# A mixture-of-experts kernel on one Trainium2 core: the gathers of the third and fourth pass moved ahead of the 16 list stores in GpSimd's order

## The chip, the core and the metric

The kernel runs on one core of one Trainium2 chip. The core has TensorE (matrix products, PE in the profile), VectorE (DVE), ScalarE (ACT), GpSimd (POOL) and SyncE (SP), and 16 DMA engines that carry the transfers that SyncE, ScalarE and GpSimd issue. The metric is the device time of one execution in microseconds (us); lower is better. One execution under the hardware profiler gives the trace that is read here.

## What is computed

Two transformer-like blocks on 512 tokens of 1024 features. The part that matters here is the mixture of experts that ends the first block: each token goes to 4 of 32 experts, an expert is a product with a 1024 x 2048 matrix, a clipped gated activation and a product with a 1024 x 1024 matrix, and the results come back weighted by the router's gates.

```
logits = xf @ w_router + b_router
top_val, top_idx = lax.top_k(logits, 4)
gates = softmax(top_val)
...
hu = xb @ w_up[e] + b_up[e]
x_glu = minimum(hu[:, :D_FF], 7.0); x_lin = clip(hu[:, D_FF:], -7.0, 7.0)
act = x_glu * sigmoid(1.702 * x_glu) * (x_lin + 1.0)
y = act @ w_down[e] + b_down[e]
...
x = x + gate2 * sum over a token's 4 experts of gate * y
```

Ahead of it stand an adaptive norm, a gated delta rule, a sliding-window attention and their output product; behind it a second block of attention, two feed-forward nets of 4096 features and a recurrent net. All weights and activations are float32.

## The kernel before

The program is written engine by engine: each engine has its own list of instructions and runs it in order; semaphores tie them together. The weights of the experts (12 MB each, some 400 MB in all) stream from HBM through six slots of 2 MB in `slots`. SyncE issues the loads (`load`, L165): each waits until TensorE has freed the slot it goes to.

**Routing.** `route_dve` (L1294 to L1434) ranks the experts by their number of tokens and works out, on VectorE, four tables: `xsl` (which row of `h2_dram` each place of an expert takes, ready with the semaphore `places` at L1380), `ysl` (where its result goes), `sloti` (for each of the 16 token-and-choice columns its place in a list by expert, L1413, ready with `route_step` 6) and `tab` (the experts of the left-over blocks and where their list starts, L1433, ready with `blocks_listed`). The last needs a short product on TensorE, `route_blocks_pe`, which runs behind the first pass.

**Passes.** The experts by rank are worked through in 31 passes in the fixed order `RANKS = (14, 15, 0, 27, 28, 16, 1, ...)`. A rank has a fixed capacity in units of 32 tokens: passes 0 and 1 (ranks 14, 15) have 2 units, pass 2 (rank 0) has 6, passes 3 and 4 (ranks 27, 28) have 1, pass 5 has 2, pass 6 (rank 1) has 5. Two units make one quad, and each quad is one gather of 64 rows of 4 KB. Tokens that don't fit an expert's capacity go to left-over blocks behind the passes; these read their tokens and their result's places from `list_dram`.

**TensorE.** `moe_pe` does `turn_x(0)`, and then for each pass i: `up(i)` (L1645, L1647), `turn_x(i + 1)` (L1621: it waits for the gather of pass i + 1 and transposes its rows), `down(i - 1)` (L1681 to L1693), `turn_act(i)` (L1659). VectorE and ScalarE carry the activation, and VectorE copies each quad's result out of PSUM (`y_out`, L1816 to L1820). So pass 2 is gathered for `turn_x(2)`, which stands between `up(1)` and `down(0)`.

**GpSimd.** `moe_pool` issues every gather (`moe_gather`, L1545), every scatter of results (L1585) and the list (L1573): 16 indirect stores of 128 rows of 12 bytes each into `list_dram`. Buffer i % 4 of `xg` takes the rows of pass i, so the gathers of passes 0 to 3 need no buffer to be freed; the gather of pass i + 4 stands at the head of step i of the loop that follows and waits for `xg_free`. `settle` (L1533 to L1536) is a one-element addition and a drain: the next instruction of GpSimd starts when the engine has nothing under way. It stands at the head of each `moe_gather`. The list is needed late: L1588 waits for it four passes from the end.

The buffer of pass 2 is `work[:, 7168:8192]`, whose first half is also `ohs`, read last by VectorE at L1411, ahead of `route_step` 6. The buffer of pass 3 is `work[:, 0:1024]`, which holds routing tables until `blocks_listed`.

Of the kernel before, what the change touches and what calls it, by code (L numbers as in the profile page):

```python
# [107 lines left out]
def build(nc, A, out, dbg=None):  # L108
# [3 lines left out]
    def S(name):  # L112
        if name not in sems:
            sems[name] = ctx.enter_context(nc.semaphore(name))
        return sems[name]

    with ctx:
# [1343 lines left out]
        def quads(i):  # L1461

            return [(q, min(UNITS[RANKS[i]] - 2 * q, 2), QBASE[RANKS[i]] + q) for q in range(QUADS[RANKS[i]])]
# [69 lines left out]
        def settle(g):  # L1533

            g.tensor_tensor(tick[:, 1:2], tick[:, 0:1], tick[:, 0:1], ALU.add)
            g.drain()  # L1536

        def moe_gather(g, i):
            if i >= 4:
                g.wait_ge(S("xg_free"), i - 3)  # L1540
            settle(g)
            for q, units, at in quads(i):
                n = units * UNIT
                to = xg[i % 4][q * 64:q * 64 + n] if q < 2 else xg_rest[0:n]
                g.indirect_dma_start(to, None, h2_dram, bass.IndirectOffsetOnAxis(ap=xsl[0:n, at:at + 1], axis=0),  # L1545
                                     bounds_check=T - 1, oob_is_err=False).then_inc(S(f"xg_in{i % 4}"), 16)

        def block_list(g, b, n):

            row = g.value_load(tab[0:1, bass.ds(b + (E + MAXO), 1)] if n is None else tab[0:1, E + MAXO + b:E + MAXO + b + 1], min_val=0, max_val=LROWS - BLK)  # L1550
            g.dma_start(idxA[:], list_dram[bass.ds(row, BLK), :]).then_inc(S("block_list"), 16)
            rows = list_dram[bass.ds(row, BLK), :].rearrange("(u r) c -> u r c", u=2)
            for u in range(2):
                for h in range(2):
                    g.dma_start(idxB[64 * u + 32 * h:64 * u + 32 * h + 32], rows[u, :, 1 + h:2 + h]).then_inc(S("block_list"), 16)

        def block_gather(g):
            settle(g)
            g.indirect_dma_start(xg[3][0:BLK], None, h2_dram, bass.IndirectOffsetOnAxis(ap=idxA[:, 0:1], axis=0)).then_inc(S("block_x"), 16)

        def moe_pool(g):
            g.memset(tick[:], 0.0)
            g.drain()
            g.wait_ge(S("places"), 1)
            g.wait_ge(S("h2_out"), 16 * TT)
            moe_gather(g, 0)
            g.wait_ge(S("biases"), 1)
            moe_gather(g, 1)
            g.wait_ge(S("list_filled"), 16)
            g.wait_ge(S("route_step"), 6)  # L1570
            settle(g)
            for j in range(TT * TOPK):
                g.indirect_dma_start(list_dram, bass.IndirectOffsetOnAxis(ap=sloti[:, j:j + 1], axis=0),  # L1573
                                     pairs[:, 3 * j:3 * j + 3], None, bounds_check=E * T - 1, oob_is_err=False).then_inc(S("list_out"), 16)
            moe_gather(g, 2)
            g.wait_ge(S("blocks_listed"), 1)
            moe_gather(g, 3)
            for i in range(NPASS):
                if i + 4 < NPASS:
                    moe_gather(g, i + 4)  # L1580
                for q, units, at in quads(i):
                    d, n = up_piece[i] + q, units * 2 * UNIT
                    g.wait_ge(S("y_ready"), d + 1)
                    settle(g)
                    g.indirect_dma_start(y2_dram, bass.IndirectOffsetOnAxis(ap=ysl[0:n, at:at + 1], axis=0), ybuf[0:n, d % 2], None,  # L1585
                                         bounds_check=2 * T * TOPK - 1, oob_is_err=False).then_inc(S(f"y_out{d % 2}"), 16)
                if i == NPASS - 4:
                    g.wait_ge(S("list_out"), 16 * TT * TOPK)  # L1588
                    block_list(g, 0, 0)
                    g.wait_ge(S("xg_free"), NPASS - 3)  # L1590
                    g.wait_ge(S("block_list"), 80)
                    block_gather(g)
            nb = g.value_load(tab[0:1, E + 2 * MAXO:E + 2 * MAXO + 1], min_val=1, max_val=MAXO)
            with g.Fori(0, nb) as b:
                g.wait_ge(S("y_ready"), b + (UPS + 1))
                settle(g)
                g.indirect_dma_start(y2_dram, bass.IndirectOffsetOnAxis(ap=idxB[:], axis=0), ybuf[:, UPS % 2], None,
                                     bounds_check=2 * T * TOPK - 1, oob_is_err=False).then_inc(S("block_y"), 16)
                g.wait_ge(S("block_y"), b * 16 + 16)
                settle(g)  # L1600
                g.drain().then_inc(S("block_done"), 1)
                block_list(g, b + 1, None)
                g.wait_ge(S("block_list"), b * 80 + 160)
                block_gather(g)
                g.wait_ge(S("block_x"), b * 16 + 32)
            for p in range(2):
                g.wait_ge(S(f"y_out{p}"), 16 * ((UPS + 1 - p) // 2))
# [900 lines left out]
        with nc.Block() as block:  # L2508
# [113 lines left out]
            @block.gpsimd  # L2622
            def _(g):
                def end():
                    meet(g, "pool")
                ada_pool(g); end()
                mixer_loads(g); ada_bias_loads(g); end()
                dn_moves(g); end()
                second_mods(g); mod_turned_loads(g)
                g.wait_ge(S("turned_out"), TURNED + PIECE["w"] + TT)  # L2630
                route_fill(g); route_loads(g)
                g.wait_ge(S("w_sum"), TT)
                gate_load(g, 5 * D); end()
                moe_pool(g); end()
                at_loads(g)
                g.wait_ge(S("x_done"), 1)
                gate_load(g, mods(0, 0)[2]); end()
                ln_loads(g, "a", 0, 0)
                g.wait_ge(S("x_done"), 2)
                gate_load(g, mods(0, 1)[2])  # L2640
                ln_loads(g, "b", 0, 1)
                g.wait_ge(S("x_done"), 3)
                gate_load(g, mods(1, 0)[2])
                rnn_small(g); rnn_gate_loads(g, 0); end()
                rnn2_pool(g); end()
                rnn3_loads(g); ln_loads(g, "c", 1, 0)
                g.wait_ge(S("x_done"), 4)
                gate_load(g, mods(1, 1)[2])
                ln_loads(g, "d", 1, 1); end()
# [32 lines left out]
```

## Time and profile before

| | us |
|---|---|
| median of 3 runs | 3620.05 |
| lowest and highest of them | 3616.89, 3629.53 |
| the profiled execution, time | 3626.3 |
| the profiled execution, span from first to last instruction | 3624.6 |
| TensorE busy, by the span | 3104.3 (86%) |
| VectorE, ScalarE, GpSimd busy | 868.8, 507.1, 237.3 |
| expert weights: 192 loads of 2048 KB | about 400 MB of the 646.73 MB moved |

The experts' stage runs from about 632 us (first load of an expert's weights) to about 1757 us of the span. The busy tenths of the page cut the span into 40 slices of 90.6 us. In the timeline each line is a group of instructions of one kind: start, duration, engine, line, operation, tile written and tiles read, count, and in brackets the idle time ahead of it with what ended it ("issue" is time in which the engine waited for nothing that the profile shows). In a table by stretch the columns are the busy time of each engine with its number of instructions, the granted TensorE clock as a share of the full one (1.00 is 2.4 GHz, 0.50 is 1.2 GHz), the mean busy share of the 16 DMA engines (rounding can take it a little over 1), and GB/s.

### The profile page before, as it was taken

The page shows a single profiled execution, that of the slowest core. Times are in us where ns is not written, and L with a number is a line of the kernel's source. Part 1 is how long each engine was busy: PE and PEld are TensorE (multiplying, and loading weights), DVE is VectorE, ACT ScalarE, POOL GpSimd, SP SyncE. Part 2 cuts the span into 40 slices and gives each one's busy share as a digit, 9 for nine tenths or more (in the row PEclk, how much of TensorE's full clock was granted, in tenths as well). Part 3 has the DMA queues.
Part 4 walks back from the last instruction along what each step waited for, and adds up shares of the span by engine and source line. Part 5 has one row for each costly group of instructions (what it writes and reads, how often), then busy time and mean ns, then how long its engine had stood idle before and what let it go on. Part 6 is the DMA issues. An engine that isn't in the chain of part 4 may idle for free.

```text
span 3624.6 us, 36753 instructions
## 1 busy us (share of the span) xinstructions
PE 3104.3 (86%) x15370; PEld 1381.0 (38%) x15370; DVE 868.8 (24%) x1281; ACT 507.1 (14%) x986; POOL 237.3 (7%) x336
## 2 busy tenths in 40 slices
PE   7999978598999989999575889999699625999998
PEld 3465555232333333333244434444233202444443
DVE  2224243311111111111312220002330671200003
ACT  1030131000000000000112210001100850200001
POOL 0000011201110111101000000000100220000000
PEclk8989967799999999999787899999899757999999
DMA  7108931979999999999500211112220021212110
GB/s 255 47 7 335 340 104 41 342 301 404 381 405 403 402 401 406 405 405 388 227 0 0 105 64 69 69 58 70 72 72 29 17 51 48 91 66 93 69 70 23
DMA packets 167094, 646.73 MB, mean 178 GB/s; under 512 B 20091, under 2 KB 29883, under 8 KB 126337
## 3 DMA queue, kind: packets, MB, share of 16 engines
q1 hardware_dynamic: 151138, 605.91, 43.5%
q0 software_dynamic: 13952, 35.48, 3.3%
q10 hardware_dynamic: 1856, 3.21, 0.3%
q8 instruction: 112, 1.84, 0.2%
q14 instruction: 36, 0.29, 0.0%
HBM read 630.69 MB, written 18.38 MB: 179 GB/s over the span
## 4 chain that ended last, share of the span: by engine, by line
PE 49%; issue 31%; DVE 5%; DMA 5%; POOL 3%; PEld 2%; ACT 2%; POOLq 2%; DVEq 1%; PEldq 0%; ACTq 0%; SPq 0%
PE ps L2177 12%; PE ps L2188 12%; PE ps L2305 6%; PE ps L2481 3%; PE ps L1996 2%; DMA stage<-gate_dram 2%; DMA slots<-in_ada_w_dram 2%; PE ps L2127 2%; PE ps L1104 2%; POOLq L1536 2%; PE ps L314 1%; PE ps L2018 1%; POOL work L1545 1%; PEld ps L434 1%; PE ps L2030 1%
## 5 line engine op out<-in xcount | busy, mean ns | idle before, releaser
L1645 PE MATMUL ps<-slots,hT 128*32 128x512 f32 x5120 | 580.3, 598 | 18.3 <-DMA slots<-in_w_up_dram 7.6
L2177 PE MATMUL ps<-hT,slots 128*128 128x512 f32 x1024 | 448.9, 599 | 13.1 <-ACT hT L975 6.6
L2188 PE MATMUL ps<-slots,work 128*128 128x512 f32 x1024 | 441.8, 593 | 12.2 <-DVE work L2225 12.2
L1645 PEld LDWEIGHTS ps<-slots,hT 128*32 128x32 f32 x5120 | 160.6, 110 | 413.3 <-issue 396.6
L2177 PEld LDWEIGHTS ps<-hT,slots 128*128 128x128 f32 x1024 | 195.3, 192 | 265.9 <-issue 265.9
L2188 PEld LDWEIGHTS ps<-slots,work 128*128 128x128 f32 x1024 | 193.7, 190 | 258.8 <-issue 247.5
L1681 PE MATMUL ps<-slots,work 128*32 128x512 f32 x2112 | 254.5, 608 | 26.1 <-DMA slots<-in_w_down_dram 19.2
L2305 PE MATMUL ps<-hT,slots 128*96 128x512 f32 x512 | 223.7, 598 | 26.3 <-DVEq L2311 24.4
L2481 PE MATMUL ps<-slots,work 96*128 96x512 f32 x256 | 112.6, 602 | 107.4 <-DVE work L2468 107.4
L1796 DVE TENSOR_SCALAR stage<-ps 128x512 f32<-128x512 f32 (+1 forms) x47 | 32.2, 686 | 581.5 <-PE ps L1647 581.1
L1681 PEld LDWEIGHTS ps<-slots,work 128*32 128x32 f32 x2112 | 90.4, 112 | 157.9 <-issue 124.6
L2305 PEld LDWEIGHTS ps<-hT,slots 128*96 128x96 f32 x512 | 83.5, 164 | 166.0 <-issue 166.0
L2216 ACT ACTIVATE stage<-ps 128x512 f32<-128x512 f32 x64 | 38.2, 597 | 759.6 <-PE ps L2177 759.6
L2225 DVE TENSOR_TENSOR work<-stage 128x512 f32<-128x512 f32 x64 | 44.3, 693 | 400.1 <-ACT stage L2216 400.1
L1774 ACT ACTIVATE modA<-stage 128x512 f32<-128x512 f32 (+1 forms) x47 | 29.6, 630 | 639.1 <-DVE stage L1796 639.1
L2481 PEld LDWEIGHTS ps<-slots,work 96*128 96x128 f32 x256 | 49.2, 193 | 169.4 <-issue 169.4
L2238 DVE TENSOR_TENSOR work<-work,ps 128x512 f32<-128x512 f32 x48 | 33.0, 688 | 303.3 <-PE ps L2188 303.3
L1996 PE MATMUL ps<-slots,hT 128*128 128x512 f32 x192 | 85.6, 606 | 3.0 <-ACT hT L975 3.0
L434 PE MATMUL ps<-hT,slots 128*128 128x512 f32 x192 | 85.3, 606 | 1.9 <-DVEq L460 1.4
L1816 DVE COPY modB<-ps 128x512 f32<-128x512 f32 x33 | 22.8, 692 | 247.3 <-PE ps L1684 238.6
L314 PE MATMUL ps<-slots,modA 128*32 128x512 f32 x512 | 65.9, 629 | 14.1 <-DMA slots<-in_ada_w_dram 10.0
L2359 PE MATMUL ps<-work 96*96 96x512 f32 x64 | 42.1, 745 | 39.3 <-ACT slots L2381 24.6
(547 smaller groups left out, 2980.2 us busy)
## 6 DMA issues: line engine op xcount, KB each, us to landing
slots<-in_w_up_dram SPq DMA_DIRECT2D x128, 2048.0 KB, 18.6
slots<-in_w_down_dram SPq DMA_DIRECT2D x64, 2048.0 KB, 17.3
slots<-in_mlp_w_dram SPq DMA_DIRECT2D x32, 2048.0 KB, 8.6
slots<-in_ada_w_dram SPq DMA_DIRECT2D x16, 2048.0 KB, 9.5
slots<-in_w_ada_dram SPq DMA_DIRECT2D x12, 2048.0 KB, 8.6
slots<-in_ada_w_dram SPq DMA_DIRECT2D x16, 1024.0 KB, 7.0
slots<-in_rnn_w_in_dram SPq DMA_DIRECT2D x8, 1536.0 KB, 6.9
slots<-in_w_in_dram SPq DMA_DIRECT2D x5, 2048.0 KB, 17.4
```

The lines of the kernel that those rows point to most:

```text
L314: ins = pe.matmul(ps[32 * j:32 * j + 32, 6 + g % 2], ada_c[:, which, 2 * q + kk], ada_slots[:, s, kk, j * CH:(j + 1) * CH], start=q + kk = ...
L434: ins = pe.matmul(ps[:, m], slots[:, s, k, m * P:(m + 1) * P], hT[:, k, :], start=k == 0, stop=k == KT - 1)
L1104: ins = pe.matmul(ps[:, 2 * (t % 2) + h], hT[:, k, t * P:(t + 1) * P], slots[:, 4 + h, k], start=k == 0, stop=k == KT - 1)
L1536: g.drain()
L1645: ins = pe.matmul(to, x[:, k, unit * UNIT:(unit + 1) * UNIT], upw[s][:, k % 2, col:col + CH], start=k == 0, stop=False)
L1681: ins = pe.matmul(to, actT[:, 4 * q + j, 64 * u + 32 * h:64 * u + 32 * h + 32], downw[sl[h]][:, j, half * CH:(half + 1) * CH], start=k == ...
L1996: ins = pe.matmul(ps[:, i % 4], hT[:, k, t * P:(t + 1) * P], slots[:, s, k], start=k == 0, stop=k == KT - 1)
L2127: ins = pe.matmul(ps[:, 2 * (t % 2) + h], hT[:, k, t * P:(t + 1) * P], slots[:, 4 + h, k], start=k == 0, stop=k == KT - 1)
L2177: ins = pe.matmul(ps[:, m], slots[:, s, k, m * P:(m + 1) * P], hT[:, k, :], start=k == 0, stop=k == KT - 1)
L2188: ins = pe.matmul(ps[:, 4 + 2 * (t % 2) + h], h1T[:, k, t * P:(t + 1) * P], slots[:, 2 + h, k], start=k == 0, stop=k == KT - 1)
L2305: ins = pe.matmul(ps[0:RW, m], slots[:, s, k, m * RW:(m + 1) * RW], hT[:, k, :], start=k == 0, stop=k == KT - 1)
L2481: ins = pe.matmul(ps[:, 2 * (t % 2) + h], xr[:, n, t * P:(t + 1) * P], slots[0:RW, s0 + n // 8, n % 8], start=n == 0, stop=n == RB - 1)
```

## The change

In `moe_pool`, GpSimd's order is changed. Behind the gather of pass 1 it waits for `route_step` 6 and gathers pass 2, waits for `blocks_listed` and gathers pass 3; only then it waits for the list's filling and issues the 16 stores. The single `settle` that stood ahead of the stores goes: each `moe_gather` has its own. Nothing else is changed.

```diff
             moe_gather(g, 0)
             g.wait_ge(S("biases"), 1)
             moe_gather(g, 1)
+            g.wait_ge(S("route_step"), 6)
+            moe_gather(g, 2)
+            g.wait_ge(S("blocks_listed"), 1)
+            moe_gather(g, 3)
             g.wait_ge(S("list_filled"), 16)
-            g.wait_ge(S("route_step"), 6)
-            settle(g)
             for j in range(TT * TOPK):
                 g.indirect_dma_start(list_dram, bass.IndirectOffsetOnAxis(ap=sloti[:, j:j + 1], axis=0),
                                      pairs[:, 3 * j:3 * j + 3], None, bounds_check=E * T - 1, oob_is_err=False).then_inc(S("list_out"), 16)
-            moe_gather(g, 2)
-            g.wait_ge(S("blocks_listed"), 1)
-            moe_gather(g, 3)
             for i in range(NPASS):
                 if i + 4 < NPASS:
                     moe_gather(g, i + 4)
```

## Rows read from the trace of the kernel before

**Rows 1.** The page: granted clock and DMA share in 40 slices.
```profile
PEclk8989967799999999999787899999899757999999
DMA  7108931979999999999500211112220021212110
```

**Rows 2.** Waits of TensorE between 690 and 720 us: total, times, longest.
```profile
PE ps L1621 <- DMA work<-h_dram,xsl: 14.7, 1, 14.7
```

**Rows 3.** Timeline of TensorE, 600 to 860 us: start, duration, what.
```profile
681.12 1.12 PE L1659 MATMUL ps<-ident,work 128*128 128x128 f32 x4 [4.44 <-DVE work L1805]
...
699.07 0.61 PE L1647 MATMUL ps<-work 96*32 96x512 bf16 x8
714.42 3.01 PE L1621 MATMUL ps<-ident,work 128*128 128x128 f32 x16 [14.74 <-DMA work<-h_dram,xsl]
717.69 8.60 PE L1681 MATMUL ps<-slots,work 128*32 128x512 f32 x64 [0.26 <-issue]
...
727.79 42.34 PE L1645 MATMUL ps<-slots,hT 128*32 128x512 f32 x384 [0.41 <-DVE modB L1816]
...
771.64 0.71 PE L1621 MATMUL ps<-ident,work 64*128 64x64 f32 x8
772.61 7.38 PE L1681 MATMUL ps<-slots,work 128*32 128x512 f32 x64 [0.26 <-issue]
...
790.86 0.71 PE L1621 MATMUL ps<-ident,work 64*128 64x64 f32 x8
...
826.06 0.61 PE L1688 MATMUL ps<-work 96*32 96x512 bf16 x2 [2.70 <-DMA slots<-in_w_down_dram]
```

**Rows 4.** Timeline of GpSimd, 560 to 1040 us.
```profile
663.46 0.95 POOL L1545 DMA_INDIRECT work<-h_dram,xsl  x1 [0.92 <-issue]
665.34 0.18 POOL L1535 TENSOR_TENSOR tick<-tick 1x1 f32<-1x1 f32 x1 [0.93 <-DVE work L1414]
673.22 1.04 POOL L1573 DMA_INDIRECT list_dram<-pairs,work  x1 [7.70 <-issue]
...
692.92 0.97 POOL L1573 DMA_INDIRECT list_dram<-pairs,work  x1 [0.30 <-issue]
693.92 0.18 POOL L1535 TENSOR_TENSOR tick<-tick 1x1 f32<-1x1 f32 x1
700.45 0.96 POOL L1545 DMA_INDIRECT work<-h_dram,xsl  x1 [6.35 <-issue]
...
715.34 0.94 POOL L1545 DMA_INDIRECT work<-h_dram,xsl  x1 [11.23 <-issue]
...
719.02 0.91 POOL L1545 DMA_INDIRECT work<-h_dram,xsl  x1 [2.54 <-issue]
```

**Rows 5.** Gathers (L1545) issued from 695 to 708 us: durations ns, time to landing.
```profile
L1545 POOL DMA_INDIRECT work<-h_dram,xsl x3: 933/952/958, 700.4 to 703.0; - x3
...
DMA to landing us min/median/max: 8.7/10.0/11.4
```

**Rows 6.** Timeline of VectorE, 655 to 800 us: last routing step.
```profile
677.72 0.40 DVE L1433 TENSOR_SCALAR tab<-work 1x64 int32<-1x64 f32 x1
```

**Rows 7.** Weight load (L165) issued in 697 to 705 us: its start, time to landing.
```profile
L165 SPq DMA_DIRECT2D slots<-in_w_up_dram x1: 372/372/372, 699.2 to 699.2; - x1
...
DMA to landing us min/median/max: 17.0/17.0/17.0
```

**Rows 8.** Table by stretch of the experts' stage.
```profile
671.00:687.00 16.00, 11.37 (x86) 4.11 (x90) 4.40 (x13) 1.69 (x3) 10.73 (x11) 0.79 1.01 393
```

**Rows 9.** The same table, later stretches.
```profile
712.00:725.00 13.00, 10.21 (x72) 4.57 (x76) 0.00 (x0) 1.76 (x3) 2.03 (x3) 0.69 0.30 92
...
735.00:780.00 45.00, 44.22 (x416) 13.59 (x408) 7.74 (x12) 2.37 (x4) 0.97 (x1) 1.00 0.59 217
780.00:822.00 42.00, 40.36 (x364) 12.84 (x364) 4.79 (x7) 3.14 (x6) 5.93 (x9) 1.00 1.02 389
...
980.00:1200.00 220.00, 210.08 (x1906) 66.77 (x1902) 30.46 (x46) 14.52 (x27) 22.51 (x36) 0.99 1.02 404
```

## Prediction

> **What bounds the kernel now.** I read four views, in this order. First the page in 40 slices: the DMA share is 9 tenths from slice 10 on to slice 19 and lower in slices 7 to 9 [rows 1]. In the experts' stage the weights' stream is the limit, save in a stretch at its head. Second, the waits of TensorE at that head: one wait of 14.7 us, by `turn_x(2)` on the gathered rows of pass 2 [rows 2]. Third, the timelines of TensorE and GpSimd there: `up(1)` ends at about 699.7 (its last group starts at 699.07 and takes 0.61), and `turn_x(2)` starts at 714.42 [rows 3]. GpSimd comes to the gather of pass 2 only at 700.45, because it issues the 16 list stores from 673.22 to 693.9, and the `settle` behind them holds it until about 699.7 [rows 4]. Last, the table by stretch: the DMA engines are busy 0.30 of the time from 712 to 725 and 0.59 from 735 to 780, and 1.02 from 780 on [rows 9]. So up to 780 TensorE sets the time, not the stream: the loads wait for slots that TensorE hasn't freed. From 780 on the stream is full, and at 826.06 TensorE waits for a weight for the first time since [rows 3].
>
> The reader is to see one chain: GpSimd's stores, gather 2, `turn_x(2)`, `down(0)`, `up(2)`, the slots that these free, the loads into them, and then the full stream to the stage's end at 1757.
>
> **The change, part by part.**
>
> *Gather 2, moved ahead.* `route_step` 6 is there when GpSimd has issued gather 1: its `settle` starts at 665.34 and lets the next DMA go at 673.22 [rows 4]. That is where the first store stands now; gather 2 takes its place. Its three DMAs start 1.26 us apart, at 673.2, 674.5 and 675.7. The same three landed 8.7 to 11.4 us after their issue [rows 5], when the DMA engines were full too, so the last lands at about 675.7 + 11.4 = 687.1. The DMA share between 671 and 687 is 1.01 [rows 8], so I take that duration and no shorter one. It is needed at 699.7: there are 12 us in hand. As a bound from above: gather 1, of one DMA, held its `settle` until about 672.4, some 9 us from its issue at 663.46 [rows 4]; three times this in a row gives 673.2 + 27 = 700.2, half a microsecond late. So the wait of 14.7 us goes, or all but 0.5 of it.
>
> *What is late next.* Behind `up(1)`, `turn_x(2)` starts at once, as `turn_x(3)` does at 771.64 behind `up(2)` [rows 3]: 714.42 - 699.7 = 14.7 us earlier. ScalarE must finish one sigmoid before it takes out the transposes, so it may lose some tenths; I take 0 to 0.8. `down(0)` needs weights that were issued before 676 and `up(2)` needs four loads of which the last was issued at 699.2 and landed 17.0 us later, at 716.2 [rows 7]. `up(2)` will start near 711.6 and works through four slots in 42.3 us [rows 3], so it comes to the last one some 32 us in, at 743. No weight is late.
>
> *The clock.* TensorE runs `down(0)` in 8.60 us now, with a granted clock of 0.69 on average over 712 to 725, that is partly at the 1.2 GHz level, behind its 14.7 us of idleness; the same 64 products at 772.61 take 7.38 with the clock at 1.00 [rows 3, 9]. Without the pause `down(0)` gains 1.2 us. A pause of 4.44 us at 681 stays as it is [rows 3]. The clock's gain is between 0 (if the transposes' short pauses bring it down anyway) and 1.5; I take 1.2.
>
> *The sum at `up(2)`.* 14.7 + 1.2 + 0.3 for the transposes' own speed = 16.2 us earlier: 727.8 becomes 711.6. Bounds: 13.9 (0.8 lost on ScalarE, nothing from the clock) and 16.8.
>
> *From there to the stream.* `up(2)` itself already runs at clock 1.00 [rows 9], so it keeps its 42.3 us. What frees slots from here to 780 is TensorE alone, so each load goes out 16.2 us earlier. Is the stream able to take them? From 712 to 780 the DMA engines are idle 13 x 0.70 + 45 x 0.41 = 9.1 + 18.5 = 27.6 us [rows 9]. The same bytes fit in a stretch shorter by 16.2 us, with 11.4 us of idleness left. So the point where the stream becomes full moves from about 780 to about 764. Behind it stream and TensorE hand over to each other as before, and everything moves by the same 16.2 us to the end of the span: nothing in the program goes by an absolute time.
>
> *The stores, moved back.* Gather 3 comes behind `blocks_listed`, at 678.1 [rows 6], but its `settle` holds it until gather 2 has landed, about 687, so the new wait costs nothing. Gather 3 goes at about 688, the 16 stores from 689.2. They take 673.22 to 699.7 now, 26.5 us until the `settle` behind them lets go [rows 4]; so they are through at about 716, and gather 4 follows at 716 to 720 (719.02 now). Gather 3 is needed at 771.64 - 16.2 = 755.4 and gather 4 at 790.86 - 16.2 = 774.7 [rows 3]: over 50 us in hand for both. Behind gather 4 stands the first scatter of results; `up(3)` and `up(4)` don't need it, and VectorE wants its buffer again only with the first quad of pass 2's results, past 790. The list itself is read past 1600. The stores' packets now meet the loads for `up(2)`, which have tens of us in hand.
>
> *The settle that goes.* It cost 7.9 us of GpSimd's time, until gather 1 had landed; the `settle` in gather 2 costs the same. Nothing is gained or lost.
>
> Sum: -16.2 us. The profiled execution (3626.3) would give 3610.1; against the median, which lies 6.3 lower, 3620.05 - 16.2 = 3603.9.
>
> **The rivals.**
>
> *A: the stream swallows it.* The stage moves a fixed number of bytes, and over 980 to 1200 it does so at 404 GB/s with the DMA engines at 1.02 [rows 9]. If the stream had no slack at the head, TensorE's earlier start would only be a longer wait at 826 and the time would be 3620. Against it stand the 27.6 us of DMA idleness just where the gain arises. A partial form: only the idleness from 712 to 725 goes (9.1 us) and the rest is a wait again; that gives 3611. The Trainium skill ("SBUF — State Buffer", section "A bandwidth-pool intuition that's wrong (but worth ruling out)") holds HBM to be almost always the end-to-end bottleneck; taken at its word, the rule gives no change here. The trace agrees with it behind 780 and not before.
>
> *B: gather 2 lands late.* By the slow rate above it lands at 700.2. VectorE is busy 4.40 us from 671 to 687 [rows 8]; if each of these held GpSimd up as well, it would land at 704.6, TensorE would wait 4.9 us and lose the clock again (1.2): 16.2 - 6.1 = 10.1, or 3610. The landing of three gathers in 11.4 us speaks against it. The Trainium skill ("SBUF — State Buffer", section "🔬 SBUF: two separate sides") says that some VectorE copies keep GpSimd from writing its DMAs' descriptors; the 4.40 us above bound what that could do here.
>
> *C: the stores make GpSimd late, and the kernel is slower.* Behind the stores stand gather 4 and every later gather and scatter. If each store held the next until it had landed, at gather 1's 9 us, 16 of them would end at 689 + 144 = 833, gather 4 would land at 836, and `turn_x(4)` would start 45 us later than the 790.9 of now: about 3665. It decides from (791 - 689 - 3) / 16 = 6.2 us a store. Against it: the stores go out 1.3 us apart now, with the DMA engines as full [rows 4, 8], and all 16 take 26.5 us.
>
> **How the numbers follow.** Forecast 0.81, A 0.10 (half of it the partial form), B 0.06, C 0.03. The forecast's own range is 13.9 to 16.8 us of gain, with 3 us on either side for the spread of the runs (3616.9 to 3629.5): 3600 to 3609. Taken to rival B and the partial form of A, and some way down for a tail that gains from a higher clock: 3598 to 3612. A measurement of this kernel can tell about 0.3%, 10.9 us, from no change; so the bound of faster is 3609.2. Faster: the forecast nearly whole, 0.80. Same: A, B and the forecast's edge, 0.16. Slower: C and what is unnamed, 0.04.
>
> **What the profile after would show.** The wait at L1621 is gone or under 1 us; the gather of pass 2 is issued at 673 and lands by 690; the first store is issued near 689 and gather 4 near 717; `down(0)` takes 7.4 us and `up(2)` starts near 711.6; the DMA idleness between 700 and 765 is some 11 us; the first wait for a down weight comes near 810; the stage ends near 1741. The prediction is wrong if `up(2)` starts on time and the span does not follow: then the waits for weights behind 810 have grown, and rival A holds. It is wrong in another way if the wait at L1621 stays (B), or if a wait for gather 4 appears near 775 (C).

## The result, and the profile after

The changed kernel takes 3629.59 us (median of 19 runs, 3621.78 to 3636.77) against 3620.88 us of the kernel before, measured beside it (19 runs, 3611.19 to 3632.43). The ratio is 1.0023, with a 95% interval of 1.0015 to 1.003: a little slower, where 16 us less was forecast. The profiled execution took 3623.17 us, span 3621.5. As the experiments show, this is one of two answers that the same pair of kernels gives, and on six numbered chips the answer went with the chip. The chip of this first measurement isn't on record, nor is that of the trace of before that the prediction rests on.

The page of the changed kernel, granted clock and DMA share in 40 slices, answers to [rows 1]:

```profile
PEclk8989977799999999999787999999899757999999
DMA  7109922889999999999500211111220021212110
```

As before, the unbroken run of nines in the DMA share begins in slice 10. TensorE at the head of the stage, answers to [rows 3] (start, duration, what, idle time before it and its releaser; x32 is one slot of weights of `up(1)`; the code behind the change stands one line higher than before, so L1645 is now L1644, and the stores are L1575):

```profile
673.84 1.11 PE L1658 MATMUL ps<-ident,work 128*128 128x128 f32 x4 [4.90 <-DVE work L1804]
674.88 9.08 PE L1644 MATMUL ps<-slots,hT 128*32 128x512 f32 x64
687.45 5.34 PE L1644 MATMUL ps<-slots,hT 128*32 128x512 f32 x32 [3.49 <-issue]
704.41 5.91 PE L1644 MATMUL ps<-slots,hT 128*32 128x512 f32 x32 [11.63 <-issue]
710.44 0.61 PE L1646 MATMUL ps<-work 96*32 96x512 bf16 x8
710.98 1.09 PE L1620 MATMUL ps<-ident,work 128*128 128x128 f32 x8
...
713.95 7.38 PE L1680 MATMUL ps<-slots,work 128*32 128x512 f32 x64 [0.26 <-issue]
```

The wait of 14.7 us at `turn_x(2)` is gone, as forecast (710.98 follows 710.44 at once), and `down(0)` takes 7.38. But inside `up(1)`, which ran through before, there are two new pauses, 3.49 and 11.63 us, put down to "issue": the profile shows nothing that was waited for. Each lies at the end of a slot, where `up` has `pe.drain().then_inc(freed[s], 1)`. GpSimd in the same record, answers to [rows 4], and SyncE, which issues a load when a slot is freed:

```profile
678.85 0.93 POOL L1545 DMA_INDIRECT work<-h_dram,xsl  x1 [7.74 <-issue]
680.08 1.03 POOL L1575 DMA_INDIRECT list_dram<-pairs,work  x1 [0.31 <-issue]
...
699.33 0.97 POOL L1575 DMA_INDIRECT list_dram<-pairs,work  x1 [0.30 <-issue]
...
703.00 0.94 POOL L1545 DMA_INDIRECT work<-h_dram,xsl  x1 [2.49 <-issue]
```
```profile
687.55 0.37 SPq L165 DMA_DIRECT2D slots<-in_w_up_dram  x1
...
704.52 0.37 SPq L165 DMA_DIRECT2D slots<-in_w_up_dram  x1
```

The pauses lie in the time of the 16 stores, and the last one ends 5.1 us behind the start of the last store. SyncE's loads go out 0.1 us after TensorE goes on, so the increments that free the slots are as late as the products behind them. The records of `up`'s drain itself (L1650) show the same; here is that of the third slot in this record (16.0 us from 688.3) and in e12_after, a record without pauses (2.8 us):

```profile
L1650 PEldq DRAIN  x1: 16008/16008/16008, 688.3 to 688.3; - x1
```
```profile
L1650 PEldq DRAIN  x1: 2790/2790/2790, 692.1 to 692.1; - x1
```

The products of that slot end at 687.45 + 5.34 = 692.8, and the drain, which ends with the increment, at 688.3 + 16.0 = 704.3. The weights of the slot behind it had landed by 674.3. So TensorE isn't waiting for a weight; its own drain with its increment isn't done. The table by stretch (duration, busy us of each engine, granted clock, DMA share, GB/s) shows what that does to the stream; it is to be read beside [rows 9]:

```profile
687.00:700.00 13.00, 5.34 (x32) 1.33 (x32) 0.00 (x0) 0.00 (x0) 9.95 (x11) 0.69 0.73 280
700.00:712.00 12.00, 7.47 (x48) 2.33 (x48) 0.90 (x2) 0.17 (x1) 1.43 (x3) 0.62 0.58 193
```

With no slot freed, the DMA engines run dry (27% of 13 us and 42% of 12 us), and the granted clock falls to 0.69 and 0.62, that is in part to 1.2 GHz.

Executions start the stage at different times, so from here on I count from gather 0, the first gather of the stage (647.1 in the profiled run of before, 639.4 in this one). `up(2)` starts 80.7 us behind gather 0 before and 722.83 - 639.4 = 83.4 behind it now. The first step of the combination behind the stage (L1872, L1873 before) comes at 1117.2 and 1120.4. Behind that, 1860 to 1862 us are left in every record of every kernel here. So the change acts between gather 0 and the end of the stage, and most of it shows at the start of `up(2)`.

### The profile page after: what moved, and what is told of

It is laid out like the page before. It is cut to its first block, busy times and chain, and to the rows that moved or that the text cites. A ratio compares the mean times of both kernels' runs of the same rounds, so it can differ in the third digit from the quotient of the medians.

```text
span 3621.5 us, 36750 instructions
## 1 busy us (share of the span) xinstructions
PE 3095.5 (85%) x15370; PEld 1376.3 (38%) x15370; DVE 868.6 (24%) x1281; ACT 506.9 (14%) x986; POOL 237.0 (7%) x335
## 4 chain that ended last, share of the span: by engine, by line
PE 46%; issue 36%; DMA 4%; DVE 4%; POOL 3%; PEld 2%; ACT 2%; POOLq 2%; DVEq 1%; PEldq 0%; ACTq 0%; SPq 0%
PE ps L2176 12%; PE ps L2187 12%; PE ps L2304 6%; PE ps L2480 3%; PE ps L1995 2%; DMA stage<-gate_dram 2%; PE ps L2126 2%; POOLq L1536 1%; PE ps L314 1%; DMA slots<-in_ada_w_dram 1%; POOL work L1545 1%; PE ps L2017 1%; PEld ps L434 1%; PE ps L2029 1%; PE ps L245 1%
## 5 line engine op out<-in xcount | busy, mean ns | idle before, releaser
L1644 PE MATMUL ps<-slots,hT 128*32 128x512 f32 x5120 | 584.0, 602 | 33.9 <-issue 15.7
L1644 PEld LDWEIGHTS ps<-slots,hT 128*32 128x32 f32 x5120 | 161.3, 111 | 432.0 <-issue 414.8
L2304 PEld LDWEIGHTS ps<-hT,slots 128*96 128x96 f32 x512 | 83.4, 164 | 166.1 <-issue 166.1
L314 PE MATMUL ps<-slots,modA 128*32 128x512 f32 x512 | 64.2, 616 | 13.5 <-DMA slots<-in_ada_w_dram 9.0
## 6 DMA issues: line engine op xcount, KB each, us to landing
slots<-in_w_up_dram SPq DMA_DIRECT2D x128, 2048.0 KB, 19.2
```

Of the source, the lines that this page charges most:

```text
L314: ins = pe.matmul(ps[32 * j:32 * j + 32, 6 + g % 2], ada_c[:, which, 2 * q + kk], ada_slots[:, s, kk, j * CH:(j + 1) * CH], start=q + kk = ...
L1644: ins = pe.matmul(to, x[:, k, unit * UNIT:(unit + 1) * UNIT], upw[s][:, k % 2, col:col + CH], start=k == 0, stop=False)
L2304: ins = pe.matmul(ps[0:RW, m], slots[:, s, k, m * RW:(m + 1) * RW], hT[:, k, :], start=k == 0, stop=k == KT - 1)
```

## The experiments

All kernels compute the whole of the reference. Each table gives the median, the ratio to the kernel before on the same chip with its interval, and from the profiled run: `up(2)` behind gather 0, the stretch of the stores behind gather 0 (first start to last start), and TensorE's pauses from the start of `turn_act(1)` to the end of `up(1)` or behind it, where a record has any beyond the usual ones.

### The changed kernel again, and three other places for the stores

Edits, against the changed kernel. "settle" lets GpSimd run empty ahead of the stores:

```diff
             g.wait_ge(S("list_filled"), 16)
+            settle(g)
             for j in range(TT * TOPK):
```

"pass 1" and "late" move the stores into the loop, behind the gather at its head, at i = 1 and i = 4:

```diff
-            g.wait_ge(S("list_filled"), 16)
-            for j in range(TT * TOPK):
...
             for i in range(NPASS):
                 if i + 4 < NPASS:
                     moe_gather(g, i + 4)
+                if i == 1:
+                    g.wait_ge(S("list_filled"), 16)
+                    for j in range(TT * TOPK):
...
```

> The changed kernel once more, for a second trace. In the first, TensorE stands still twice inside up(1), 3.5 us behind k=3 and 11.6 us behind k=5, though the weights it waits for had landed before 675. Theory 1 (the pauses belong to the order of this kernel): they come again at the same two places, 15 us in all, and up(2) starts about 85 us behind the first gather. Rival (a chance event of one execution): no pause, up(2) starts 70 us behind the first gather, and the time is near 3604. Timed: 1.001 to 1.003 of the kernel before by theory 1.

> The changed kernel with the settle put back ahead of the 16 stores, behind gather 3; the stores then start about 7 us later. Theory 1a (the stores stop TensorE because they are sent while gather 3 is still under way, which the order before never did): the pauses of 15 us vanish, the time is 3604 to 3607. Theory 1b (the stores stop TensorE through what they do themselves, in this stretch): the pauses stay, moved by some 7 us with the stores, and the time is 3625 to 3632.

> The changed kernel with the 16 stores moved further back, behind gather 5 and ahead of the scatter of pass 1's results: they run beside up(2), 192 products without a wait for a new gather, with the DMA engines idle 0.41 of the time. Theory 1a and 1b with the weights' stream needed for the pause: no pause in up(1) and none in up(2), 3604. Theory 1c (the stores stop TensorE wherever they run): the pauses of some 15 us appear in up(2), 3620 to 3630. In each case up(1) has no pause if the stores cause it; if it has, the stores are not the cause.

> The changed kernel with the 16 stores at the head of pass 4's results (behind gather 8): they run near 820 to 850 us, where the weights' stream is full and TensorE waits for it. If the stores cause the pause in up(1), up(1) is clean and up(2) starts 16 us earlier than before, 3604. By theory 1c a pause of some 15 us appears near 830, half hidden by the waits for weights: 3605 to 3612. If the pause in up(1) stays, the early gather itself is the cause, not the stores: 3620 to 3630.

| run (chip 8) | median us | ratio | `up(2)` | stores | pauses |
|---|---|---|---|---|---|
| e1_after | 3614.19 | 0.996 [0.9948, 0.9972] | 64.2 | 39.9 to 59.5 | none |
| e2_settle | 3610.68 | 0.9951 [0.9939, 0.9963] | 64.1 | 46.1 to 65.8 | none |
| e3_pass1 | 3612.04 | 0.9945 [0.9932, 0.9958] | 64.3 | 74.4 to 93.6 | none |
| e4_late | 3615.96 | 0.9961 [0.9948, 0.9973] | 64.3 | 189.9 to 209.3 | none |

The changed kernel itself is 0.4% faster here, with no pause at all, so nothing could be told of the stores' place. The kernel before has a median of 3629.97 on this chip, not 3620, so the times near 3604 that were expected for the three other places weren't met (3610.7 to 3616.0). What differs is not the kernel. The same kernel was then run on other chips.

> The changed kernel, unaltered, on what may be another chip. Theory R (the pauses of 15 us inside up(1) depend on the chip or on how the program lies on it, and decide the sign of the change): where TensorE has no pause the time is 0.995 to 0.997 of the kernel before, where it has them 1.001 to 1.003; both can come. Rival (the pauses were one event of the first measurement): no pause and 0.996 again.

Chip 12: 3632.18 against 3620.27, ratio 1.0026 [1.0009, 1.0042], with the pauses back. TensorE in this record:

```profile
681.66 5.03 PE L1644 MATMUL ps<-slots,hT 128*32 128x512 f32 x32
686.90 3.64 PE L1644 MATMUL ps<-slots,hT 128*32 128x512 f32 x32 [0.21 <-issue]
695.53 4.93 PE L1644 MATMUL ps<-slots,hT 128*32 128x512 f32 x32 [4.99 <-issue]
710.41 6.01 PE L1644 MATMUL ps<-slots,hT 128*32 128x512 f32 x32 [9.95 <-issue]
```

Again 15 us in all, again at the ends of slots, and again the last ends 5.1 us behind the start of the last store (705.28). `up(2)` is at 83.4. The loss isn't that of the traced execution alone: the fastest of the 10 executions here took 3619.55 us, and the slowest of the 15 of this kernel on chips 8, 10 and 11 took 3619.6.

### The stores against gather 3

One reading was that the pause needs gather 3 still under way when the stores begin. "g3behind" takes it out of their way:

```diff
             moe_gather(g, 2)
-            g.wait_ge(S("blocks_listed"), 1)
-            moe_gather(g, 3)
             g.wait_ge(S("list_filled"), 16)
+            settle(g)
             for j in range(TT * TOPK):
...
+            g.wait_ge(S("blocks_listed"), 1)
+            moe_gather(g, 3)
```

> The changed kernel with a settle ahead of the 16 stores, again, to meet a chip of the kind where the changed kernel has its pauses (there the kernel before takes some 3620, on the other kind some 3630). Theory 1a (the stores stop TensorE because they are sent while gather 3 is under way; the order before never did that): no pause, some 0.996 of the kernel before on either kind. Theory 1b (the stores stop TensorE by what they do beside up(1)): pauses inside up(1) or in what follows it, 1.001 to 1.003 on the pausing kind, 0.996 on the other.

> The changed kernel with the 16 stores behind gather 5, beside up(2), again, for the same reason. Theory 1a: the stores follow gather 5 at once, so a gather is under way, and on the pausing kind TensorE pauses inside up(2): 1.000 to 1.003. Theory 1b with a full weights' stream needed: no pause, as the stream is idle 0.41 of the time there: 0.995. Theory 1c (the stores stop TensorE wherever they run): pauses in up(2), 1.000 to 1.003. On the other kind 0.995 by all.

> The changed kernel once more, beside two variants of it on the same chip. Two kinds of execution have been seen: with two pauses inside up(1) (up(2) starts 83.4 us behind gather 0, time 1.002 to 1.003) and without (64.2 us, 0.996). If the kind is a property of the chip, chips not met so far may show either.

> Gather 2 ahead of the stores, gather 3 behind them as before, and a settle between gather 2 and the first store: the stores start some 39 us behind gather 0, one us ahead of the changed kernel's, but with no gather under way. Only of use where the changed kernel of this call pauses. Theory 1a (a gather under way when the stores are sent): no pause, 64.2 us, 0.996. Theory 1b (the stores beside this part of up(1)): the pauses are there, 80 to 84 us, 1.001 to 1.003. Where the changed kernel doesn't pause: 0.996 by both.

> The settle between gather 3 and the stores, for the third time: first store 46 us behind gather 0. Where the changed kernel of this call pauses: theory 1a says no pause and 0.996; theory 1b says pauses of the same size, later inside up(1) or behind it, 1.001 to 1.003. Elsewhere 0.996.

> The kernel before, for a second trace: its time differs from chip to chip (3620 where the changed kernel pauses, 3626 to 3633 where it doesn't). Theory K (the kernel before has pauses of its own on the chips where the changed one has none): up(2) starts more than the 80.7 us behind gather 0 seen so far, or the stage's end more than 1117.2. Rival: both are the same and the difference of 10 us lies in the blocks outside the experts' stage, ahead of gather 0 (647.1 so far) or behind the stage.

> The changed kernel on the same chip as the two variants that follow. With pauses inside up(1): up(2) 83.4 us behind gather 0, 1.002 to 1.003 of the kernel before, which is then near 3620. Without: 64.2 us and 0.994 to 0.996, the kernel before at 3626 to 3633.

> Stores behind gather 2 and a settle, 38.7 us behind gather 0, no gather under way. Where the changed kernel of this call pauses: theory 1a (a gather under way) 64.2 us and 0.995, theory 1b (the stores at this time) 80 to 84 us and 1.002. Elsewhere 0.994 to 0.996.

> Stores behind gather 3 and a settle, 46 us behind gather 0. Where the changed kernel of this call pauses: theory 1a 64.2 us and 0.995, theory 1b 80 to 84 us and 1.002. Elsewhere 0.994 to 0.996.

> The settle between gather 3 and the stores once more, sent alone in the hope of the chip on which the changed kernel paused (29 executions of it on that kind gave 1.002 to 1.003; on three other chips 0.994 to 0.996). There theory 1a (a gather under way when the stores are sent) says up(2) 64.2 us behind gather 0 and 0.995 of the kernel before; theory 1b (the stores beside the end of up(1)) says 80 to 84 us and 1.001 to 1.003. On the other chips 64.2 us and 0.995.

| run | chip | median us | before | ratio | `up(2)` | pauses us |
|---|---|---|---|---|---|---|
| e6_settle | 10 | 3613.7 | 3626.21 | 0.996 [0.9945, 0.9975] | 64.3 | none |
| e7_pass1 | 10 | 3611.13 | 3626.21 | 0.9949 [0.9931, 0.9967] | 64.9 | none |
| e8_after | 10 | 3609.71 | 3632.53 | 0.9937 [0.9918, 0.9956] | 64.3 | none |
| e9_g3behind | 10 | 3610.87 | 3632.53 | 0.9939 [0.992, 0.9958] | 64.6 | none |
| e10_settle | 10 | 3611.28 | 3632.53 | 0.9945 [0.9926, 0.9964] | 64.2 | none |
| e11_before | 11 | 3630.44 | 3627.11 | 1.0005 [0.9994, 1.0016] | 83.0 | none |
| e12_after | 11 | 3614.06 | 3627.11 | 0.9964 [0.995, 0.9978] | 64.4 | none |
| e13_g3behind | 11 | 3611.83 | 3627.11 | 0.9954 [0.9938, 0.9971] | 64.9 | none |
| e14_settle | 11 | 3611.3 | 3627.11 | 0.9949 [0.9932, 0.9966] | 64.2 | none |
| e15_settle | 6 | 3631.95 | 3622.49 | 1.0021 [1.0008, 1.0034] | 83.4 | 7.9 and 7.4 |

On chips 10 and 11 every form is 0.4 to 0.6% faster and none has a pause; the forms can't be told apart. On chip 6 the form with `settle` is slower by 0.2%, so a gather under way is not needed. In its record `settle` put the stores 6 us later, and the pauses moved with them, out of the middle of `up(1)` to its end and behind it. The 7.9 us lie ahead of the products with the bias (L1647), which take no slot of weights; the 7.4 us are a wait for ScalarE, which in turn waits for VectorE's late step. TensorE of e15_settle, and VectorE and GpSimd beside it:

```profile
696.80 3.64 PE L1645 MATMUL ps<-slots,hT 128*32 128x512 f32 x32 [0.18 <-issue]
708.33 1.05 PE L1647 MATMUL ps<-work 96*32 96x512 bf16 x8 [7.89 <-issue]
709.31 1.97 PE L1621 MATMUL ps<-ident,work 128*128 128x128 f32 x8
718.68 1.11 PE L1621 MATMUL ps<-ident,work 64*128 64x64 f32 x8 [7.40 <-ACT hT L1765]
```
```profile
716.80 0.69 DVE L1796 TENSOR_SCALAR stage<-ps 128x512 f32<-128x512 f32 x1 [34.03 <-remote]
```
```profile
693.90 1.04 POOL L1576 DMA_INDIRECT list_dram<-pairs,work  x1 [6.09 <-issue]
...
713.15 0.97 POOL L1576 DMA_INDIRECT list_dram<-pairs,work  x1 [0.30 <-issue]
```

This record shows more of what is late. VectorE's L1796 waits for `up_ready`, which the last product of L1647 raises. That product is done at 708.33 + 1.05 = 709.4; in a record without the pause (e14_settle) VectorE starts at the end of it. Here it starts at 716.80, 7.4 us later, though TensorE had gone on to its transposes meanwhile. So it is not TensorE's arithmetic that stands still but what it signals: its increments of semaphores reach the others, and in the case of a drain let TensorE itself go on, some microseconds late while the stores are under way. What delays an increment isn't shown.

A count in the traces goes with it. The 16 stores raise `list_out` 256 times (16 each). Of these the records of e5_again, e15_settle and the first measurement of the change hold 42 to 44; all records without a pause hold 224 to 256. Completions of weight loads are missing in the same stretch too, so the count marks the records with the pause and doesn't say which transfers cause it.

### The kernel before on such a chip

Open was whether the kernel before pauses too, where the change loses.

> The kernel before, unchanged. In runs of the changed kernel and of the one that lets GpSimd settle first, TensorE stood still for 15 to 16 us in up(1) and in front of the steps behind it while the 16 stores went out, in three of nine records (up(2) 83.4 us behind gather 0 instead of 64.2 to 64.9). Theory A: the pause belongs to the chip and to the stores wherever they run, so the kernel before has it too, in up(1) or ahead of it, and its wait of 14.7 us for gather 2 only becomes shorter by it: where the kernel before is timed at 3620 to 3623, its record shows at least 5 us of idle time inside up(1) or in the steps around it, a wait by turn_x(2) below 10 us, and up(2) still 80 to 84 us behind gather 0. Theory B: the pause needs the new place of the stores: up(1) runs through in 17 us, the wait by turn_x(2) is 14 to 17 us. If it is timed at 3626 or more and up(1) is whole, the chip is of the other kind and the run tells only its own time.

> The 16 stores a pass later, behind gather 5, 74 to 94 us behind gather 0, beside up(2). Theory A (the pause follows the stores wherever they run): where the kernel before is timed at 3620 to 3623, up(1) is whole, up(2) starts 64 to 65 us behind gather 0, and the record shows pauses of together 10 to 16 us inside up(2) or just behind it; the median is 3625 to 3635, ratio 1.000 to 1.004. Theory B (it needs this place beside up(1)): no pause, median 3604 to 3610, ratio 0.995 to 0.996. Where the kernel before is timed at 3626 or more, both give 3611 to 3613 and 0.9945 to 0.995, as measured twice.

> The kernel before, unchanged, once more. Theory A: where the changed kernel stands still beside its stores, the kernel before does so too, hidden under its wait for gather 2: on such a chip (the kernel before timed at 3620 to 3623 so far) its record shows idle time of at least 5 us inside up(1), only 40 to 50 of the 256 completions of the stores, and a wait by turn_x(2) below 10 us with up(2) still 80 to 84 us behind gather 0. Theory B: the pause needs the new place, so up(1) runs through in 17 us there and the wait is 14 to 17 us. On a chip timed at 3626 or more both give a whole up(1) in 17 us, a wait of 14 to 17 us and up(2) at 80 to 83 us, as three records have shown.

| run | chip | median us | before | ratio | `up(2)` | pauses us |
|---|---|---|---|---|---|---|
| e16_before | 1 | 3628.43 | 3630.13 | 0.9996 [0.9984, 1.0008] | 80.2 | none |
| e17_pass1 | 1 | 3611.37 | 3630.13 | 0.9946 [0.9926, 0.9966] | 64.3 | none |
| e18_before | 12 | 3620.06 | 3623.45 | 0.9994 [0.9983, 1.0005] | 74.2 | 6.3 and 7.0 |

The first two fell on a chip without the pause and repeat what was known. The third fell on chip 12. TensorE of e18_before:

```profile
680.98 1.09 PE L1659 MATMUL ps<-ident,work 128*128 128x128 f32 x4 [6.25 <-issue]
682.00 4.64 PE L1645 MATMUL ps<-slots,hT 128*32 128x512 f32 x32
693.68 13.13 PE L1645 MATMUL ps<-slots,hT 128*32 128x512 f32 x96 [7.04 <-issue]
706.92 0.61 PE L1647 MATMUL ps<-work 96*32 96x512 bf16 x8
707.46 1.10 PE L1621 MATMUL ps<-ident,work 128*128 128x128 f32 x8
```

GpSimd there:

```profile
670.79 1.04 POOL L1573 DMA_INDIRECT list_dram<-pairs,work  x1 [7.28 <-issue]
...
690.50 0.97 POOL L1573 DMA_INDIRECT list_dram<-pairs,work  x1 [0.30 <-issue]
...
694.11 0.96 POOL L1545 DMA_INDIRECT work<-h_dram,xsl  x1 [2.44 <-issue]
```

ScalarE takes out the transposes of `turn_x(1)`, which TensorE ended at 674.02 + 0.71 = 674.7:

```profile
680.76 0.58 ACT L1765 COPY hT<-ps 128x512 f32<-128x512 f32 x1 [2.33 <-remote]
```

The kernel before pauses as well: 6.25 us ahead of `turn_act(1)` (where 4.2 to 4.4 are usual), and 7.04 in `up(1)`. TensorE's signal to ScalarE is 6.0 us late here, while VectorE's, amid the same stores, reaches ScalarE at once (the sigmoid of L1774 starts at 677.80, where VectorE's L1796 ends at 677.8). Only 47 of 256 completions are recorded. And it pays nothing at `turn_x(2)`: the wait of [rows 2] doesn't exist on this chip, since `up(1)` ends at 707.5 instead of 699.7, and gather 2 is in by then: it is issued 49.0 us behind gather 0, for 53.4 in [rows 4], since the `settle` behind the stores takes 2.44 us instead of 6.35. The stream had run dry in the pause (686 to 694 in the table by stretch), and that the short `settle` comes of it is argued, not tried:

```profile
686.00:690.00 4.00, 0.64 (x8) 0.00 (x0) 0.00 (x0) 0.00 (x0) 3.08 (x4) 1.00 0.19 60
690.00:694.00 4.00, 0.32 (x4) 0.21 (x8) 0.00 (x0) 0.00 (x0) 1.35 (x3) 0.61 0.01 0
```

The expectation that came true is theory A, but for one number: it had `up(2)` still at 80 to 84, and it came at 74.2.

So there are two answers. Counted against `up(2)` at 64.2 to 64.4, which the changed kernel reaches on chips 8, 10 and 11:

| | kernel before | changed | difference | ratio of the times |
|---|---|---|---|---|
| chips 8, 10, 11 (1 for before) | 80.2 to 83.0 | 64.2 to 64.4 | -16 to -19 | 0.9937 to 0.9964 |
| chips 12, 6 and the first measurement's | 74.2 | 83.4 | +9.2 | 1.0021 to 1.0026 |

In the lower row the 83.4 is that of three records, the changed kernel twice and "settle" once, and the 74.2 that of e18_before alone. Chips 10 and 12 were each met twice and gave the same answer both times. The medians follow: 3632.18 - 3620.27 = +11.9 on chip 12 and +8.7 in the first measurement, against 9.2 here; at the end of the stage the two records of chip 12 are 13.5 us apart (1124.3 and 1110.8 behind gather 0). The kernel before is itself faster on the chips with the pause (3620.27, 3622.49, 3623.45 against 3626.21 to 3632.53), as `up(2)` is 6 to 9 us earlier there.

## Why the prediction was wrong

*What bounds the kernel.* Right for the trace of [rows 2 to 4], which has no pause, and not where the result was measured. The one record of the kernel before on such a chip (e18_before) has no wait for gather 2 at all: the pause sets the time of the stretch.

*Gather 2 and its wait.* Right. On chip 11 (e12_after) it is issued at 672.78 (forecast 673.2), and its three DMAs land in 7.7 to 9.7 us, so by 684.9 (687.1). TensorE and the landings of that record:

```profile
681.63 16.91 PE L1644 MATMUL ps<-slots,hT 128*32 128x512 f32 x128
698.65 0.61 PE L1646 MATMUL ps<-work 96*32 96x512 bf16 x8
699.19 1.09 PE L1620 MATMUL ps<-ident,work 128*128 128x128 f32 x8
701.19 0.71 PE L1620 MATMUL ps<-ident,work 64*128 64x64 f32 x8 [0.91 <-ACT hT L1764]
702.16 7.38 PE L1680 MATMUL ps<-slots,work 128*32 128x512 f32 x64 [0.26 <-issue]
...
711.04 24.43 PE L1644 MATMUL ps<-slots,hT 128*32 128x512 f32 x220 [0.41 <-DVE modB L1815]
```
```profile
DMA to landing us min/median/max: 7.7/9.0/9.7
```

*ScalarE, the clock, the sum.* Right there, or nearly: 0.91 us lost to ScalarE (bound 0.8), 7.38 for `down(0)`, `up(2)` at 711.04 (711.6). Against gather 0 that is 64.4 instead of 80.7: 16.3 us for a forecast of 16.2. That the two agree to 0.1 is in part luck: beside the kernel before on the same chip (e11_before, 83.0) it is 18.6 us. The upper bound of 16.8 doesn't follow from its terms either, which add up to 14.7 + 1.5 + 0.3 = 16.5.

*The stream takes it.* Nearly right. In e12_after the DMA share says:

```profile
712.00:725.00 13.00, 12.90 (x124) 4.29 (x120) 0.00 (x0) 0.00 (x0) 2.31 (x4) 1.00 1.02 396
725.00:735.00 10.00, 9.89 (x96) 2.98 (x92) 0.00 (x0) 0.00 (x0) 0.98 (x1) 1.00 0.80 286
735.00:765.00 30.00, 29.10 (x280) 9.50 (x268) 8.43 (x13) 3.00 (x6) 0.18 (x1) 1.00 0.67 246
```

Idle are 10 x 0.20 + 30 x 0.33 = 11.9 us (forecast 11), and the first wait for a down weight is at 809.14 (810). Nothing of the gain goes to the stream: between `up(2)` and the end of the stage TensorE waits 33.4 us for weights, for 33.1 in the trace of before, and the last of the 31 `up` ends 16.5 us earlier against gather 0 (e12_after, then before; these are its products with the bias):

```profile
1668.22 0.83 PE L1646 MATMUL ps<-work 96*32 96x512 bf16 x12
```
```profile
1685.13 0.83 PE L1647 MATMUL ps<-work 96*32 96x512 bf16 x12
```

At the end of the stage 14.0 are left (1103.2 against 1117.2 behind gather 0). The 2.5 us are lost behind the last `up`, beside the left-over blocks; the reason wasn't looked for, and it isn't rival A.

*The stores, moved back.* This is the step that failed. The first store starts at 687.10 there (forecast 689.2) and gather 4 at 713.46 (717): the times were right. Wrong was the sentence that the stores' packets meet only loads that have tens of us in hand, by which the move cost nothing. I asked what the stores share with the loads, and not what goes on with TensorE's signals beside them. On chips 12 and 6 TensorE's increments are late in each of the three stretches in which the stores were tried there (25.7 to 45.4, 40.5 to 59.7 and 46.1 to 65.3 us behind gather 0). In the kernel before (e18_before) 2.1 of the 6.25 us are new and so are the 7.04: with 0.9 us of slower products `up(2)` comes 9.9 us later than it could (74.2 for 64.3). In the changed kernel it is 3.49 + 11.63 = 15.1 us, with 0.7 ahead of them (4.90 for 4.17) and 3.4 of slower products (9.08 + 5.34 + 5.91 = 20.33 for 16.91): 19.2 us by these terms, 19.1 by `up(2)` (83.4 for 64.3). So on such a chip the old place costs 9.9 us, and gather 2 is hidden behind them at no cost of its own; the new place costs 19.1, and the change makes the stretch 9.2 us longer where 16.2 less was forecast.

*The rivals.* B didn't occur. C suspected the stores rightly, as far as the times tell, and had the victim wrong: the stores, 1.27 us apart as before, held up no transfer that TensorE waited for; it is TensorE's increments that are late beside them. The mark set for C, a wait for gather 4, would have missed it.

*The clock* cost 3.4 us in the pauses, a price the forecast had only as a gain.

*Settled and open.* Shown is that the pause is in the kernel before too, that it moves with the stores, that it doesn't need gather 3, and that all three records from chips 12 and 6 have it, while none of the 15 from chips 1, 8, 10 and 11 has. Why the chips differ isn't known. That the increments themselves are late is read from the drains and from the engines that wait for them, in four records. That the stores cause it rests on the times alone: no run on such a chip has `up(1)` without stores beside it. And they may not be the whole cause: the drain of `turn_x(1)` ends before the first store of the changed kernel and takes 3.3, 2.4 and 2.2 us in the three records with the pause, for 1.7 to 1.8 in all without, while gather 2 is going out. Whether the recording itself takes part isn't known either. Why the new place costs 19 and the old 10 is argued: in the old one the first half of the stores falls into 674 to 681, where TensorE waits for VectorE anyway. Whether the stores are harmless beside `up(2)` or later on a chip with the pause was not measured; "pass 1" ran three times (0.9945, 0.9949, 0.9946), each time on a chip without it. No form beat the changed kernel by more than the intervals.

## What to carry to other kernels

When a wait is taken away, ask what else was lying under it: an engine that stands in a wait can hide a disturbance that shows only when the wait has gone. When work is moved off one queue's critical place, look at what it does to engines that share no data with it, here at small indirect stores with many completions beside an engine that has to signal every 4 us. And measure a gain of half a per cent on more than one chip: here the sign went with the chip.

## What the runs showed that was not expected

- While 16 indirect stores (128 rows of 12 bytes) went out 1.27 us apart, TensorE stood still at its drains for 3.5 to 11.6 us at a time, and an increment by one of its products reached VectorE 7.4 us late. This came in the first measurement of the change and on chips 12 and 6 only.
- The same kernel before has a median of 3620 to 3623 us on chips 12 and 6 and of 3626 to 3633 on chips 1, 8, 10 and 11. The faster chips are those with the pause: there it lies where TensorE would wait for gather 2 anyway, gather 2 lands 61.8 us behind gather 0 for 67.3 in the first trace, and `down(0)` runs in 7.38 us for 8.60.
- GpSimd's `settle` behind the stores lasted 6.35 us with the stream full, and 2.44, 2.49, 2.49 and 4.12 us in the four records with the pause.
